# Rows of the split `h` and `act` tiles padded by 16 bytes in a hybrid SSD, pooling and conv-FFN trunk

## What is computed

```python
def conv_ffn(u, w_up, conv_w, conv_b, w_down):        # D_MODEL 1024, D_FF 2816
    h = causal_depthwise_conv(u @ w_up, conv_w, conv_b)
    gate, val = jnp.split(h, 2, axis=-1)
    return (jax.nn.silu(gate) * val) @ w_down

for i in range(2):
    h = rms_norm(x, norm_mix_pre[i])
    mix = ssd_mixer(h, ...) if i % 2 == 0 else pool_mixer(h, ...)
    x = x + rms_norm(mix, norm_mix_post[i])
    f = conv_ffn(rms_norm(x, norm_ffn_pre[i]), ffn_w_up[i], ...)
    x = x + rms_norm(f, norm_ffn_post[i])
```

## The kernel before

| tiles | remainder by 128 bytes |
|---|---|
| `h_hi`, `h_lo`, `raw`, `w_hi`, `w_lo` | 0 |
| `act_hi`, `act_lo`, `y_hi`, `y_lo`, `wf_hi`, `wf_lo`, `wdt_hi`, `wdt_lo`, `stage` | 96 |

## Time and profile before

### The profile page before, as it was taken

The page is one execution under the profiler, slowest core; times in us unless marked ns, Lnnn a source line. Parts: engine busy times, 40 slices in busy tenths (PEclk is TensorE's granted clock), DMA queues, the critical chain, the costliest instruction groups (busy, mean ns, idle before and its releaser), DMA issues.

```text
span 1215.5 us, 14906 instructions
## 1 busy us (share of the span) xinstructions
PE 1169.0 (96%) x5868; PEld 976.5 (80%) x5868; DVE 671.3 (55%) x770; ACT 523.1 (43%) x613; POOL 17.5 (1%) x76
## 2 busy tenths in 40 slices
PE   5999999999999899999999999997999999999997
PEld 5877888888788697888888888887888888888885
DVE  4568776868733546556566421377556556562124
ACT  4476666666422443444434211254444434441112
POOL 5000000000000000000000000000000000000000
PEclk9999999999999999999999999998999999999999
DMA  8243333333322404322332322412232333223211
GB/s 274 69 125 102 107 126 105 127 103 124 98 95 74 139 1 139 98 90 88 104 104 94 114 77 96 156 35 70 82 103 75 104 104 103 95 78 106 103 70 69
DMA packets 85229, 122.28 MB, mean 101 GB/s; under 512 B 4150, under 2 KB 71198, under 8 KB 85182
## 3 DMA queue, kind: packets, MB, share of 16 engines
q1 hardware_dynamic: 84592, 121.37, 30.3%
q10 hardware_dynamic: 590, 0.25, 0.1%
HBM read 119.44 MB, written 2.16 MB: 100 GB/s over the span
## 4 chain that ended last, share of the span: by engine, by line
PE 90%; DVE 5%; ACT 3%; DMA 1%; issue 1%; SPq 0%; DVEq 0%; ACTq 0%
PE bank L857 25%; PE bank L267 19%; PE bank L269 19%; PE bank L268 19%; PE bank L635 2%; DVE w_lo L264 1%; PE bank L644 1%; PE bank L620 1%; ACT w_hi L259 1%; DMA raw<-in_ssd_w_in 1%; DVE stage L299 1%; DVE xres L302 1%; PE bank L1018 1%; PE bank L598 1%; PE bank L331 1%
## 5 line engine op out<-in xcount | busy, mean ns | idle before, releaser
L267 PE MATMUL bank<-h_hi,w_hi 128*128 128x512 f32 (+1 forms) x1056 | 403.9, 382 | 12.9 <-DVE h_lo L343 9.3
L269 PE MATMUL bank<-h_hi,w_lo 128*128 128x512 f32 (+1 forms) x1056 | 400.1, 379 | 0.0
L268 PE MATMUL bank<-h_lo,w_hi 128*128 128x512 f32 (+1 forms) x1056 | 399.5, 378 | 0.0
L264 DVE TENSOR_TENSOR w_lo<-raw,w_hi 128x2048 fp32r<-128x2048 f32 x92 | 210.7, 2291 | 243.8 <-ACT w_hi L259 243.8
L378 DVE SCALAR_TENSOR_TENSOR tmp<-bank,par,tmp 128x511 f32<-128x511 f32 (+2 forms) x248 | 185.2, 748 | 129.5 <-ACT tmp L369 116.6
L259 ACT ACTIVATE w_hi<-raw 128x2048 fp32r<-128x2048 f32 x92 | 175.3, 1905 | 176.2 <-PE bank L857 158.1
L267 PEld LDWEIGHTS bank<-h_hi,w_hi 128*128 128x128 f32 x1056 | 201.0, 190 | 51.1 <-DVE w_lo L264 7.5
L269 PEld LDWEIGHTS bank<-h_hi,w_lo 128*128 128x128 f32 x1056 | 200.7, 190 | 36.9
L268 PEld LDWEIGHTS bank<-h_lo,w_hi 128*128 128x128 f32 x1056 | 201.1, 190 | 35.5
L369 ACT ACTIVATE tmp<-bank,par 128x512 f32<-128x512 f32 x112 | 86.5, 774 | 268.4 <-PE bank L269 268.3
L857 PE MATMUL bank<-w_lo,act_hi 128*128 128x512 f32 x352 | 110.7, 395 | 0.0
(11 more groups left out here) (158 smaller groups left out, 970.2 us busy)
## 6 DMA issues: line engine op xcount, KB each, us to landing
raw<-in_ffn_w_up SPq DMA_DIRECT2D x44, 1024.0 KB, 5.0
raw<-in_ffn_w_down SPq DMA_DIRECT2D x22, 1024.0 KB, 4.9
raw<-in_ssd_w_in SPq DMA_DIRECT2D x20, 1024.0 KB, 5.5
decay<-ac_dram SPq DMA_DIRECT2D x16, 512.0 KB, 3.5
raw<-in_ssd_w_out SPq DMA_DIRECT2D x8, 1024.0 KB, 4.9
from_start<-ac_dram SPq DMA_DIRECT2D x32, 128.0 KB, 3.8
xres<-in_x SPq DMA_DIRECT2D x4, 512.0 KB, 8.1
result<-xres SPq DMA_DIRECT2D x4, 512.0 KB, 2.6
```

What stands on the lines that cost most here:

```text
L264: dve.tensor_tensor(lo[:], raw[n % 2][:], hi[:].bitcast(F32), ALU.subtract).then_inc(lo_ready, 1)
L267: pe.matmul(dst, wh, xh, start=first, stop=False, **kw)
L268: pe.matmul(dst, wh, xl, start=False, stop=False, **kw)
L269: return pe.matmul(dst, wl, xh, start=False, stop=last, **kw)
```

## The change

A row of `h_hi`, `h_lo`, `act_hi` and `act_lo` becomes 516 floats long; the last four are never used. Block k of a tile then starts 2064 k bytes behind its first one in place of 2048 k. Everything declared behind `h_lo` moves up by 256 bytes, and `act_lo` by 608.

```diff
+SKEW = 4
...
-        h_hi = sb("h_hi", [P, DB, T], F32R)
-        h_lo = sb("h_lo", [P, DB, T], F32R)
+        h_hi = sb("h_hi", [P, DB, T + SKEW], F32R)[:, :, 0:T]
+        h_lo = sb("h_lo", [P, DB, T + SKEW], F32R)[:, :, 0:T]
...
-            act_hi = sb("act_hi", [P, FB, T], F32R, scope=scope)
-            act_lo = sb("act_lo", [P, FB, T], F32R, scope=scope)
+            act_hi = sb("act_hi", [P, FB, T + SKEW], F32R, scope=scope)[:, :, 0:T]
+            act_lo = sb("act_lo", [P, FB, T + SKEW], F32R, scope=scope)[:, :, 0:T]
```

## The result

The changed kernel takes 1228.47 us (median of 7 runs, 1226.41 to 1231.67), the kernel before, beside it, 1218.18 us (7 runs, 1216.10 to 1222.97). The ratio is 1.0084, 95% interval 1.0064 to 1.0103. The forecast was 1228.1, by losing the even step in the up products. The seven runs of the kernel before fall into two groups, four at 1216.1 to 1218.2 and three at 1222.3 to 1223.0 us, so a single run can lie some 5 us off another.

What follows compares the result with a forecast made beforehand. The prediction took TensorE's dense matmul stream, busy 96% of the span, as the bound. Its terms 9.6 + 2.9 - 1.8 - 0.8 summed to +9.9 us, from 1218.2 to 1228.1 us, with a range of 1201 to 1237.

Steps and rivals of the forecast that it cites:

- the even step: Up-stage matmuls of 512 columns starting regularly every 226.7 ns; forecast to be lost, chance 0.49.
- Up products: 1920 up-stage matmuls, forecast to go from 226.7 ns to 5.0 ns more each, +9.6 us; ends -6.1 and +12.9.
- the middle row: Up-stage estimate of +5.0 ns, from a scan block's first steps at 231.7 ns, chosen between +3.3 and +6.7.
- Scan: 36 scan groups of 24 matmuls: some 576 matmuls slow by 5.0 ns, +2.9 us; ends -1.8 and +3.9.
- Down products: 1056 down-stage matmuls, forecast to go from 233.4 to 231.7 ns, -1.8 us; bounds -7.1 and 0.
- 256 columns: 256-column blocks: two of three sets, 384 matmuls at 120.0 ns, may fall to 116.9; -0.8 us taken, -1.2 at most.
- the third set: The 256-column matmuls with stationary `wf`, at 116.9 ns before, forecast to stay there.
- Output projection: Matmuls of `y` and `w`, whose remainders are kept: forecast 0 change, 233.4 ns, the control in the new trace.
- Writes: Writes of h and act: forecast 0; 5% slower `h_lo` writes would cost the four stage starts 1.0 us together.
- part 1: The forecast's item on the 1920 up-stage matmuls, +9.6 us; it held that only block 0 keeps equal remainders.
- nothing moves: Rival: stage differences come from roles, PSUM bank or load order, not addresses; 1218 to 1220 us, chance 0.27.
- Spreading helps: Rival: walking offsets make TensorE's two reads meet less, so up, scan and down steps fall; -16.3, 1202 us, chance 0.24.

## Why the prediction was right, and where it was not

1. *Up products.* Forecast +5.0 ns for 1920 matmuls, +9.6 us. Measured 231.9 - 226.7 = 5.2 ns, +10.0 us. The value taken was the middle row, the unsettled steps of a scan block. It was the right size, and that is luck as much as reading: no row had such an offset, and constant offsets alone give anything from 228.9 to 233.5 ns. The steps are also not what that block shows: they follow the block number with a fixed pattern, on average from 228.8 ns in block 0 to 235.8 in block 6, so the upper bound of 233.4 held for the mean, and not for a single block.
2. *Scan.* Forecast +2.9 us. From the first matmul of the dt product to the first of the output projection it was 272.3 us (45.8 to 318.1) and is 274.8 (46.3 to 321.1): +2.5.
3. *Down products.* Forecast -1.7 ns, -1.8 us. Measured -1.3 ns and -1.2 us by the chain (0.54 + 0.69), -1.3 us for all 1056. The padding of `act` alone shows it apart from the rest. Counted by 256 bytes, not one block in eight has equal remainders here but blocks 2 and 18 of `act_hi` and block 12 of `act_lo`.
4. *256 columns.* Forecast -0.8 us. 384 x -2.5 ns is -1.0. But the third set, which was to stay at 116.9, did not. 24 steps of it:

```profile
447.27 0.28 PE L268 MATMUL bank<-h_hi,wf_hi 128*128 128x256 f32 x1
...
450.12 0.28 PE L268 MATMUL bank<-h_hi,wf_hi 128*128 128x256 f32 x1
```

2.85 us are 118.8 ns, and 192 x 1.9 is +0.4 us.

5. *Output projection.* 233.4 ns, unchanged.
6. *Writes.* 685 for 684 ns: nothing. TensorE's idle time went from 46.5 to 44.9 us, inside the 2 us that the prediction allowed.

The sum of the measured parts is 10.0 + 2.5 - 1.3 - 1.0 + 0.4 = 10.6 us; the medians differ by 10.3. The interval of the ratio allows 7.8 to 12.5 us, so a fit of some tenths is luck. The 12.5 us between the profiled executions are these 10.6, the 3.1 of the pooling stage less the 1.7 of the output projection, and 0.5 us elsewhere.

Two things in the working were wrong without harm to the sum. I counted remainders by 128 bytes. The period is 256, and by 256 bytes `h_lo` lies 128 away from the weights in the changed kernel, since `h_hi` ahead of it grew by 128 bytes. So not even block 0 kept its equal remainder in all passes, as part 1 had it, and it takes 228.8 ns and not 226.7. And I took each block's step to go by its own remainder, and later each matmul's by its own pair. The run with `h_lo` moved speaks against that.

Of the rivals, *nothing moves* fell with the result, which lies 8 us above its 1220, and with the constant offsets: 16 bytes in every block, with no change of offset between blocks to pay for, cost 5.0 ns. The rule of the Trainium skill that I weighed, in "TensorE: Matmul & The Clock Gate", Part 2, two independent read ports, does not carry over to the time of these `float32r` streams: four offsets of the same tiles gave 228.9 to 233.5 ns for 226.7. *Spreading helps* was right for two of the three sets of 256 columns (120.0 to 117.5 ns), where it is worth 1 us, and for the down products, whose constant 32 bytes it broke up (1.3 us); it was wrong for the up products, where most of the time is.

## What to carry to other kernels

In a dense `float32r` stream, read the distance from start to start, and where the same shape has two values in two stages, compare the addresses of the moving and the stationary tiles: here, equal remainders by 256 bytes were worth 3% of each 512-column matmul. Eight small tiles in the layout (`eps` and the seven of 64 bytes) had taken them from the down and output products, over a quarter of the program. `eps` alone is not to blame: without it the difference would be 64 bytes, which cost 2.2 ns in the up products. Spreading the rows over offsets cost 0.8% here, and the tile to move was the misaligned one.

## What was not expected of the hardware

- The step of a 512-column `float32r` matmul with a 128-column stationary tile depends on the difference of the two tiles' places by 256 bytes: 226.7 ns at 0 (and at 256), 228.9 at 64, 231.7 at 16, 233.3 at 128, 233.5 at 32.
- The difference does not settle it alone. In layer 1 the 128 bytes gave 232.3 ns, and `h_lo` moved by 32 bytes gave 233.3 in place of 231.2.
- Most of the 512-column streams settle into a short pattern that repeats, six steps long with the rows of `h_hi` padded by 128 bytes. In the scan block of the earlier trace rows the even step comes after about eight matmuls.
- One matmul in three with another difference raised the mean by two thirds of what three in three do in layer 0, and by all of it in layer 1.
- With 256 columns the equal case is no better than the others: 120.0 ns, for 116.9 at a difference of 32 bytes. It is not alone at 120.0. With `h` offset by 64 bytes the set on `wf`, whose difference is then 96, takes 2.88 us for 24 steps:

```profile
451.74 0.28 PE L268 MATMUL bank<-h_hi,wf_hi 128*128 128x256 f32 x1
...
454.62 0.28 PE L268 MATMUL bank<-h_hi,wf_hi 128*128 128x256 f32 x1
```

What meets inside the chip is open: whether the moving read disturbs the load of the next stationary tile or the other way round was not separated, nor what decides between two patterns at the same difference. For 512 columns, differences between 128 and 256 bytes were not tried alone.
